# Ordering a router's experts on the chip and giving the 14 lightest a two-pass gate product

## The chip, the cores and the metric

The kernel runs on one core of one Trainium2 chip. The metric is the device time of one execution in microseconds, lower is better. Every time here comes from timed runs or from one execution that the hardware profiler recorded.

## What is computed

One decoder layer over 1024 tokens of width 1024: a mixer (gated linear attention beside differential attention), and then a mixture of experts. The change lies in the second part, which in the reference is this:

```python
def hier_moe(x, wg, bg, we, be, w1, w3, w2):
    ...
    g_w, g_idx = lax.top_k(g_prob, 1)                    # one of 4 groups
    e_w, e_idx = lax.top_k(jax.nn.softmax(e_sel, axis=-1), TOP_K)   # 2 of its 8 experts
    expert = g_idx * EXPERTS_PER_GROUP + e_idx
    ...
    def expert_block(args):
        xb, e = args
        hdn = jax.nn.silu(xb @ w1[e]) * (xb @ w3[e])     # 1024 -> 512, twice
        return hdn @ w2[e]                               # 512 -> 1024
    ...
    out = jnp.zeros((n_tok + 1, d), f32).at[row_tok].add(y.astype(f32) * row_w[:, None])[:n_tok]
```

Each token goes to 2 of 32 experts, so a list of tokens has 64 entries on average. With these inputs the reference's router gives lists of 34 to 88 tokens; experts 0 and 1 have 42 and 44, and the 14 lightest of the other 30 have 34 to 63.

## The kernel before

All is written with explicit semaphores; each engine has a program of its own. TensorE is PE, VectorE is DVE, ScalarE is ACT, GpSimd is POOL, and SP only issues transfers.

**The front.** The mixer, the router and the lists of tokens. `place[:, e, t]` says at which slot of expert e's list a token stands, `slot_rows` what is written there (token number and weight, in bf16 parts). It fills the first half of the span.

**The expert stage** (`stage_experts`, second half). `over_experts` runs the experts 0 to 31 in their own order: 4 written out, a loop over 24 in bodies of four, 4 written out, and a tail. Each engine's program of one expert is `pe_expert`, `act_expert`, `dve_expert`, `pool_expert`, `sp_expert`. Of one expert:

- Six chunks of weights of 1 MB (128 x 2048 fp32): 0, 1 of `w1`, 2, 3 of `w2` **of the expert before** and 4, 5 of `w3`. SP fetches a chunk of expert e once DVE has read the same chunk of expert e-2 (`load_chunk`, L1772).
- Products are made in fp32r with both operands split in two. ACT rounds a chunk to its high part (`high`, L1976, into `w_high`), DVE subtracts to get the low part (`low`, L1980, into `w_low`), PE multiplies. There are three slots of high and low parts, so ACT's rounding of a chunk waits until PE has used the chunk three before (`chunk_used`).
- A product (`product`) is three matmuls: x high by w high, x high by w low, x low by w high (L2003, L2004, L2005). The list of up to 96 slots is the stationary operand, 512 columns of weights are moving: 12 matmuls a chunk, 72 an expert.
- `silu` on ACT (L1931), `hidden` on DVE (L1935, `hd`), four transposes of `hd` on PE (`h_transposes`, L1907) between the gate products of chunks 0 and 1 of the next expert, split on ACT and DVE (L2167, L2236), the two `w2` chunks, `weighted` on ACT (`main_y`, L1938), and a scatter that adds 96 rows to `out` in memory (POOL, L1926).
- Ahead of that: for expert e+4 DVE makes the one-hot matrix of the list (`pick`, L1847), for e+3 PE turns it into token numbers (L1855), DVE adds them up (`main_token`, L1865) and POOL gathers the rows of x (L1892); for e+1 PE transposes them (L1900), and ACT and DVE split them (L2209, L2214).

DVE's order in expert e is what the prediction needs: `hd` of e-1, low 2, `hT_low`, low 3, low 4, weights and destinations of a list, two `xT_low`, token numbers, low 5, low 0 of e+1, `pick` of e+4, low 1 of e+1. It ends the stage's last expert in halves (`gate_by_half`, `h_half`, `down_by_half`). A list of over 96 would be done behind the tail; none is here.

Of the kernel before, what the change touches and what calls it, by code (L numbers as in the profile page):

```python
# [49 lines left out]
CAP = 96  # L50
MORE = -(-SEQ // CAP) - 1
# [27 lines left out]
EXPERTS = {"w_high1": 20, "w_high2": 28, "xT_high0": 36, "xT_high1": 39, "xT_low0": 42, "xT_low1": 45, "sl": 48,  # L79
# [31 lines left out]
def build(nc, a):  # L111
    with ExitStack() as top:
# [6 lines left out]
        def place(name, shape, dt=F32):  # L119
# [6 lines left out]
            "ident": keep("ident", [P, P]), "causal": keep("causal", [P, HG, 64]),  # L126
            "gain_q": keep("gain_q", [P, 1]), "gain_k": keep("gain_k", [P, 1]),
            "minus_half": keep("minus_half", [P, 8]),
            "logits": keep("logits", [P, T, NG + NE]),
            "dqT": place("dqT", [P, HD, SEQ]), "dkT": place("dkT", [P, HD, SEQ]),  # L130
# [88 lines left out]
def stage_front(nc, a, s, tools):  # L219
# [70 lines left out]
    e2, gexp = sb("e2", [P, 1], kib=19.1875), sb("gexp", [P, NG], kib=19.21875)  # L290
    w, wden = sb("w", [P, 2], kib=19.25), sb("wden", [P, 1], kib=19.28125)
# [55 lines left out]
    rel_out, filled, relf_mm, rel_step = sem("rel_out"), sem("filled"), sem("relf_mm"), sem("rel_step")  # L347
    lam_step, lam_exp, masked = sem("lam_step"), sem("lam_exp"), sem("masked")
    anti_ready, turned, prepared = sem("anti_ready"), sem("turned"), sem("prepared")
# [25 lines left out]
    placed, shared, weighed, flagged = sem("placed"), sem("shared"), sem("weighed"), sem("flagged")  # L375
    own = {"dve": 0, "pool": 0}
# [113 lines left out]
    def total_counts():  # L490

        nc.vector.tensor_copy(counts[:, 0:NE], pc[0:1, :])
        nc.vector.tensor_reduce(counts[:, NE:NE + 1], pc[0:1, :], AX.X, ALU.max)
# [10 lines left out]
    def sync(sp):  # L504
# [35 lines left out]
        sp.wait_ge(masked, 1)  # L540
# [51 lines left out]
        for n in range(1, T + 1):  # L592
# [3 lines left out]
            elif n == RING + 3:  # L596
                for c in range(2):
                    load_chunk(sp, a, s, 0, 0, c)
            elif n == T:
                sp.wait_ge(g_o_mm, T)  # L600
                for c in (0, 1):
                    load_chunk(sp, a, s, 1, 1, c)
                sp.wait_ge(added, 2 * T - 1)
                for c in (4, 5):
                    load_chunk(sp, a, s, 0, 0, c)
# [7 lines left out]
    def tensor(pe):  # L613
# [253 lines left out]
        nc.tensor.matmul(pf[:, 0:REL], relb[:], onehot[:], start=True, stop=True).then_inc(relf_mm, 1)  # L867
        for i in range(T, AHEAD):
# [6 lines left out]
            if 2 in behind.get(i, {}):  # L875
                if behind[i][2] == q_units[0]:
                    pe.wait_ge(rel_step, 1)
                q_transposes(behind[i][2])
            if i == INDEX["dv", 5]:
                pe.wait_ge(q_stored, T)  # L880
                pe.wait_ge(bias_in, 16 * HD)
                pe.wait_ge(anti_ready, 1)
# [60 lines left out]
    def scalar(act):  # L943
# [177 lines left out]
        for i in range(T, AHEAD):  # L1121
# [16 lines left out]
            if i == INDEX["z", 3]:  # L1138
                act.wait_ge(lam_step, 3)
                nc.scalar.activation(lexp[:], lsum[:], ACT.Exp).then_inc(lam_exp, 1)  # L1140
# [57 lines left out]
    def gpsimd(pool):  # L1198
# [33 lines left out]
        for half in range(2):  # L1232
# [3 lines left out]
                                    pattern=[[0, HG], [1, 64]],  # L1236
# [545 lines left out]
def stage_experts(nc, a, s, tools, front):  # L1782
# [209 lines left out]
    def sp_expert(sp, e, r, j, last, tail=False):  # L1992
        if not some(e, 2):
            return
# [553 lines left out]
```

## Time and profile before

| what | us |
|---|---|
| time, median of 3 runs | 1193.33 (1191.17 to 1193.42) |
| span of the profiled execution, first to last instruction | 1187.8 |
| PE busy in it | 1140.4 (96%) |
| DVE busy | 886.6 (75%) |
| ACT busy | 693.8 (58%) |
| POOL busy | 258.4 (22%) |

The span leaves out what lies around the program, 5.5 us against the median; a change of the span is taken as a change of the time. PE's busy time counts overlapping matmuls, so that a full PE says only that it is never empty. In the second half the DMA engines are busy without a pause as well. The rows of single instructions stand further below.

### The profile page before, as it was taken

The numbers are of one execution on the slowest core, as the hardware profiler recorded it, in microseconds if no ns is written. First come the engines' busy times: TensorE is split into PE (matmuls) and PEld (weight loads), VectorE is DVE, ScalarE is ACT, GpSimd is POOL, SyncE is SP. The second block draws the span as 40 slices with busy tenths as digits, with TensorE's granted clock in tenths as the row PEclk, the third lists the DMA queues.
The fourth block names the chain that finished last, engine by engine and source line by source line (L and its number), as shares of the span: only waits on it lengthen the run. The fifth ranks groups of instructions, "written<-read, shape, count | busy, mean of one in ns | idle before, by whom it ended". The sixth has DMA issues, their size and how long they took to land.

```text
span 1187.8 us, 17134 instructions
## 1 busy us (share of the span) xinstructions
PE 1140.4 (96%) x5899; PEld 866.7 (73%) x5900; DVE 886.6 (75%) x1304; ACT 693.8 (58%) x916; POOL 258.4 (22%) x327
## 2 busy tenths in 40 slices
PE   6999999999999889999699999999999999999997
PEld 5877887767777678888467777777777777777775
DVE  4424423666577788887699989999999999998885
ACT  5424203455455643434367777777777777777774
POOL 2211102411111222223441221212212122122111
PEclk9999999999999999999799999999999999999999
DMA  8130301200200444343599999999999999999982
GB/s 321 43 107 1 106 27 45 72 27 36 98 27 9 146 146 151 127 166 121 214 400 377 387 388 374 399 378 377 392 371 384 380 369 399 374 380 387 370 293 34
DMA packets 67794, 273.34 MB, mean 230 GB/s; under 512 B 13172, under 2 KB 19896, under 8 KB 43288
## 3 DMA queue, kind: packets, MB, share of 16 engines
q1 hardware_dynamic: 57000, 245.32, 53.4%
q0 software_dynamic: 7280, 20.98, 7.8%
q10 hardware_dynamic: 3456, 6.29, 1.4%
q8 instruction: 33, 0.54, 0.2%
q14 instruction: 25, 0.20, 0.1%
HBM read 248.44 MB, written 28.32 MB: 233 GB/s over the span
## 4 chain that ended last, share of the span: by engine, by line
PE 87%; DVE 6%; POOL 2%; ACT 2%; issue 2%; DMA 1%; POOLq 0%; ACTq 0%; DVEq 0%
PE main_pm L649 12%; PE main_score L649 6%; PE main_score L2003 5%; PE main_score L2005 5%; PE main_pt L2005 5%; PE main_score L2004 5%; PE main_pt L2003 5%; PE main_pt L2004 5%; PE main_po L2005 5%; PE main_po L2004 5%; PE main_po L2003 5%; PE main_score L710 3%; PE main_po L733 2%; PE main_score L821 2%; PE main_score L823 2%; PE main_score L822 2%
## 5 line engine op out<-in xcount | busy, mean ns | idle before, releaser
L1980 DVE TENSOR_TENSOR main_w_low<-w_raw,main_w_high 128x2048 fp32r<-128x2048 f32 x189 | 432.1, 2287 | 48.9 <-ACT main_w_high L1976 48.7
L1976 ACT CAST main_w_high<-w_raw 128x2048 fp32r<-128x2048 f32 x190 | 362.5, 1909 | 75.6 <-PE main_score L2005 52.6
L1892 POOL DMA_INDIRECT main_xg<-xn_dram,main_token x32 | 76.5, 2391 | 372.1 <-DVE main_token L1865 366.4
L2003 PE MATMUL main_score<-main_w_high,main_hT_high 128*96 128x512 f32 x256 | 102.4, 400 | 0.0
L2003 PE MATMUL main_pt<-main_w_high,main_xT_high 128*96 128x512 f32 x252 | 101.0, 401 | 0.0
L2005 PE MATMUL main_score<-main_w_high,main_hT_low 128*96 128x512 f32 x256 | 100.8, 394 | 0.0
L2004 PE MATMUL main_score<-main_w_low,main_hT_high 128*96 128x512 f32 x256 | 100.4, 392 | 0.0
L2005 PE MATMUL main_po<-main_w_high,main_xT_low 128*96 128x512 f32 (+1 forms) x256 | 100.3, 392 | 0.0
L2003 PE MATMUL main_po<-main_w_high,main_xT_high 128*96 128x512 f32 (+1 forms) x256 | 99.8, 390 | 0.2 <-DVE main_w_low L1980 0.2
L2005 PE MATMUL main_pt<-main_w_high,main_xT_low 128*96 128x512 f32 x252 | 99.8, 396 | 0.0
L2004 PE MATMUL main_po<-main_w_low,main_xT_high 128*96 128x512 f32 (+1 forms) x256 | 99.7, 389 | 0.0
L2004 PE MATMUL main_pt<-main_w_low,main_xT_high 128*96 128x512 f32 x252 | 98.9, 393 | 0.0
L649 PE MATMUL main_pm<-slot_high,xh 128*128 128x512 f32 x208 | 87.2, 419 | 2.5 <-DVE slot_low L1356 2.5
L649 PE MATMUL main_pm<-slot_low,xh 128*128 128x512 f32 x208 | 82.7, 398 | 0.0
L649 PE MATMUL main_pm<-slot_high,xl 128*128 128x512 f32 x208 | 82.4, 396 | 0.0
L1926 POOL DMA_INDIRECT out<-main_y,main_dest x31 | 50.4, 1627 | 90.0 <-ACT main_y L1938 52.4
L1011 ACT ACTIVATE main_prob<-main_score,main_nmax 128x128 f32<-128x128 f32 (+7 forms) x64 | 47.5, 743 | 32.8 <-DVE main_nmax L1415 32.0
L2004 PEld LDWEIGHTS main_po<-main_w_low,main_xT_high 128*96 128x96 f32 x256 | 41.4, 162 | 17.7
L2005 PEld LDWEIGHTS main_score<-main_w_high,main_hT_low 128*96 128x96 f32 x256 | 41.2, 161 | 17.9
L2003 PEld LDWEIGHTS main_po<-main_w_high,main_xT_high 128*96 128x96 f32 x256 | 41.3, 161 | 17.5 <-DVE main_w_low L1980 0.4
L2005 PEld LDWEIGHTS main_po<-main_w_high,main_xT_low 128*96 128x96 f32 x256 | 41.3, 161 | 17.3
L2005 PEld LDWEIGHTS main_pt<-main_w_high,main_xT_low 128*96 128x96 f32 x252 | 40.6, 161 | 17.7
(329 smaller groups left out, 2333.7 us busy)
## 6 DMA issues: line engine op xcount, KB each, us to landing
w_raw<-in_moe_w SPq DMA_DIRECT2D x192, 1024.0 KB, 18.0
slot_raw<-in_w_in SPq DMA_DIRECT2D x12, 1024.0 KB, 7.4
main_x<-in_x SPq DMA_DIRECT2D x8, 512.0 KB, 11.0
slot_raw<-in_w_out SPq DMA_DIRECT2D x4, 1024.0 KB, 6.8
main_hx<-in_x SPq DMA_DIRECT2D x8, 512.0 KB, 3.8
out<-main_hx SPq DMA_DIRECT2D x8, 512.0 KB, 2.9
xn_dram<-main_xn SPq DMA_DIRECT2D x8, 512.0 KB, 2.8
gr_dram<-main_stage ACTq DMA_DIRECT2D x8, 256.0 KB, 2.0
```

Of the source, the lines that this page charges most:

```text
L649: last = nc.tensor.matmul(bank(i), stationary, moving, start=(k == 0 and n == 0), stop=(k == KD - 1 and n == 2))
L710: last[comp] = nc.tensor.matmul(score[comp][:, k0:k1], dqT[r:r + 64, h, t * P:(t + 1) * P], dkT[r:r + 64, h, k0:k1], start=True, stop=True)
L733: last = nc.tensor.matmul(po[:, 0:DDV], wT[:, j, :], dv[:, j, h * DDV:(h + 1) * DDV], start=(j == 0), stop=(j == t))
L821: nc.tensor.matmul(acc[half], hi, w_hi, start=(k == 4), stop=False)
L1011: nc.scalar.activation(out, score[comp][:, 0:nk], ACT.Exp, bias=nmax[:, n % 2, comp:comp + 1], accum_out=sums[:, n % 3, comp:comp + 1]).th ...
L1892: nc.gpsimd.indirect_dma_start(xg[u][:], None, s["xn2_dram"], bass.IndirectOffsetOnAxis(token[u][:, 0:1], 0), bounds_check=bound["x"], oob ...
L1926: nc.gpsimd.indirect_dma_start(a["out"].rearrange("b n d -> (b n) d"), bass.IndirectOffsetOnAxis(dest[v][:, 0:1], 0), y[u][:], None, bound ...
L1976: nc.scalar.copy(wh[slot(c, e)][:], raw[u][c // 2][:, c % 2, :]).then_inc(w_high, 1)
L1980: nc.vector.tensor_tensor(wl[slot(c, e)][:], raw[u][c // 2][:, c % 2, :], wh[slot(c, e)][:].bitcast(F32), ALU.subtract).then_inc(w_low, 1)
L2003: nc.tensor.matmul(out, x_hi, w_hi, start=start, stop=False)
L2004: nc.tensor.matmul(out, x_hi, w_lo, start=False, stop=False)
L2005: return nc.tensor.matmul(out, x_lo, w_hi, start=False, stop=stop)
```

## The change

After the router the 32 experts are ordered by their number of tokens: experts 0 and 1 stay first, the others follow, the heaviest first. DVE multiplies the counts by 32 and takes off the expert's number to get different keys, compares each with each, PE counts by products with ones who stands above whom, and DVE turns this into `order`. SP and POOL read `order` into a register for each expert (`ranked`, `value_load`) and take weights and lists by it. POOL copies the expert's `place` and `slot_rows` to `place_of` and `rows_of`, from which DVE's `pick` and PE's product then read (`list_rows`).

The first 18 of the order are done as before ("heavy"). The last 14 ("light") take lists of 64. Their x stands in one tile `xT_both` of 128 columns, 64 high parts beside 64 low parts, so that a gate chunk takes 8 matmuls, by `w_high` and by `w_low`, and not 12. The result has 128 rows; ACT copies both gate results to `both`, and PE multiplies them by `fold`, a matrix of zeros and ones that adds row n+64 to row n and transposes at once. ACT then takes the silu of the first, DVE multiplies, and both split the hidden values. Products with `w2` are as before; the scatter writes 64 rows.

```diff
+    def compare(dve):
+        ...
+        dve_then(dve, V.scalar_tensor_tensor(out=key[:], in0=pc[0:NE, :], scalar=float(NE), in1=s["key_bias"][0:NE, :],
+                                             op0=ALU.mult, op1=ALU.add))
+        ...
+        V.tensor_scalar(above[:], key[:], key_at[:, 0:1], None, ALU.is_lt).then_inc(order_step, 1)
...
+    xTb = [sb(f"xT_both{u}", [P, KD, 2 * LIGHT_CAP], F32R, kib=EXPERTS[f"xT_high{u}"]) for u in range(2)]
+    both = [sb(f"both{m}", [P, DE], kib=EXPERTS[n]) for m, n in enumerate(("sl", "hd"))]
...
+    def fold_mm(pe, m, by_block=False):
+        for j in range(KE):
+            h = both[m][:, j * P:(j + 1) * P] if by_block else both[m].rearrange("p (c k) -> p k c", k=KE)[:, j, :]
+            last = nc.tensor.matmul(folded[m][:, j, :], h, fold[:], start=True, stop=True)
+        return last
...
+        if isinstance(e, int) and e == 2:
+            sp.wait_ge(after["order_step"], after["ORDERED"])
+        which = None if tail else ranked(sp, e)
...
+    def ranked(eng, e):
+        return eng.value_load(s["order"][0:1, bass.ds(e, 1)], min_val=0, max_val=NE - 1)
...
+            if light:
+                nc.tensor.matmul(ph_both[c // 4], xTb[u][:, kx, :], w_hi[:, w], start=(kx == 0), stop=False)
+                last = nc.tensor.matmul(ph_both[c // 4], xTb[u][:, kx, :], w_lo[:, w], start=False,
+                                        stop=(kx == KD - 1))
...
+            act.wait_ge(chunk_used, number(e - 1, 5) + 1)
+            nc.scalar.copy(both[1][:], ph_both[1]).then_inc(q.hd, 1)
...
+    def turned_hidden(dve, e):
+        dve.wait_ge(slT_ready, folds(e))
+        nc.vector.tensor_tensor(hT[:], folded[1], slT[:], ALU.mult).then_inc(hT_ready, 1)
+        dve.wait_ge(hT_high, e)
+        nc.vector.tensor_tensor(hTl[:, :, 0:LIGHT_CAP], hT[:], hTh[:, :, 0:LIGHT_CAP].bitcast(F32),
+                                ALU.subtract).then_inc(hT_low, 1)
...
         if not last:
-            pick(q, e + 4, e + 4, u)
+            dve.wait_ge(listed_rows, e + 3)
+            pick(q, e + 4, e + 4, u, place_of[u][:])
...
+    def list_rows(pool, e, u):
+
+        which = ranked(pool, e)
+        if some(e, 4):
+            pool.wait_ge(q.ids_mm, e - 1)
+        nc.gpsimd.tensor_copy(place_of[u][:], place[:, bass.ds(which, 1), :].rearrange("p a t -> p (a t)"))
+        nc.gpsimd.tensor_copy(rows_of[u][:], rows[:, :, bass.ds(which, 1), :].rearrange(
+            "p t a r -> p t (a r)")).then_inc(listed_rows, 1)
...
         if not (tail or (last and j >= 1)):
             pool_gather(pool, e + 3, 1 - u)
+        if not last:
+            list_rows(pool, e + 4, u)
...
+        four_of(0, 0, False)
+        with eng.Fori(1, 4) as i:
+            four_of(4 * i, 2 * i, False, light=False)
+        four_of(16, 8, False)
+        with eng.Fori(5, NE // 4 - 1) as i:
+            four_of(4 * i, 2 * i, False, light=True)
+        four_of(NE - 4, NE // 2 - 2, True)
+        expert(eng, NE, NE // 2, 0, True, [True, False, False], tail=True)
```

The last expert's gate and hidden product are no longer done in halves.

**POOL, one expert in the loop.** Of before, the gather of a list and the scatter of the one that is done:

```order
L2293 REGISTER_ALU
L1890 REGISTER_ALU
L1892 DMA main_xg_167<-xn_dram,main_token_187 96x1024
L2302 ISA
L1923 ISA
L1926 DMA out<-main_y_209,main_dest_189 1024x1024
```

Of the changed kernel, where between the two a register is loaded and two copies read what the front left in SBUF:

```order
L1949 DMA main_xg_172<-xn_dram,main_token_192 96x1024
L2073 ISA
L2073 TENSOR_LOAD order
L2073 ISA x2
L2381 ISA
L2381 COPY main_place_of_219<-place 128x8
L2382 ISA
L2382 COPY main_rows_of_217<-slot_rows 128x48
L1987 REGISTER_ALU
L1990 DMA out<-main_y_225,main_dest_196 1024x1024
```

The copies stand behind the gather and ahead of the scatter; nothing of this was on POOL in the loop before.

**DVE, from low 5 of an expert to `hT_low` in the next.** Of before:

```order
L1980 TENSOR_TENSOR main_w_low_176<-w_raw_66,main_w_high_172 128x2048
L1980 TENSOR_TENSOR main_w_low_170<-w_raw_67,main_w_high_168 128x2048
L1847 TENSOR_TENSOR main_onehot_180<-iota_slot,place 128x768
L1980 TENSOR_TENSOR main_w_low_171<-w_raw_67,main_w_high_169 128x2048
L1935 TENSOR_TENSOR main_hd<-main_po,main_sl 96x512
L1980 TENSOR_TENSOR main_w_low_176<-w_raw_68,main_w_high_172 128x2048
L2236 TENSOR_TENSOR main_hT_low<-main_score,main_hT_high 128x384
```

Of the changed kernel, in the loop over light experts:

```order
L2046 TENSOR_TENSOR main_w_low_182<-w_raw_69,main_w_high_178 128x2048
L2045 ISA
L2046 TENSOR_TENSOR main_w_low_176<-w_raw_64,main_w_high_174 128x2048
L1903 TENSOR_TENSOR main_onehot_187<-iota_slot,main_place_of_219 128x768
L2046 TENSOR_TENSOR main_w_low_177<-w_raw_64,main_w_high_175 128x2048
L2045 REGISTER_ALU
L2046 TENSOR_TENSOR main_w_low_182<-w_raw_65,main_w_high_178 128x2048
L2293 REGISTER_ALU
L2294 TENSOR_TENSOR main_hT<-main_score,main_slT 128x256
L2296 TENSOR_TENSOR main_hT_low<-main_hT,main_hT_high 128x4x64
```

The one-hot matrix is now made from POOL's copy; in a light expert `hd` is gone and a product of 128x256 stands behind low 2. In a heavy expert `hd` stays where it was.

## Rows read from the trace of the kernel before

**Rows 1.** The page: busy time of each engine.

```profile
PE 1140.4 (96%) x5899; PEld 866.7 (73%) x5900; DVE 886.6 (75%) x1304; ACT 693.8 (58%) x916; POOL 258.4 (22%) x327
```

**Rows 2.** Stretches: length, busy us (instructions) of the five, PE's clock, DMA share, GB/s.

```profile
711.00:715.00 4.00, 4.00 (x19) 2.81 (x18) 3.62 (x4) 3.57 (x4) 2.51 (x2) 1.00 1.01 426
700.00:1100.00 400.00, 400.00 (x2004) 291.29 (x2004) 365.69 (x327) 307.93 (x263) 83.98 (x44) 1.00 1.02 382
```

**Rows 3.** Groups, 700 to 900 us, shapes apart: busy, mean ns, idle before and releasers.

```profile
L1980 DVE TENSOR_TENSOR main_w_low<-w_raw,main_w_high 128x2048 fp32r<-128x2048 f32 x66 | 150.9, 2287 | 16.8 <-ACT main_w_high L1976 16.8
L1976 ACT CAST main_w_high<-w_raw 128x2048 fp32r<-128x2048 f32 x66 | 126.0, 1909 | 27.0 <-PE main_score L2005 19.3 <-PE main_po L2005 7.7
...
L1847 DVE TENSOR_TENSOR main_onehot<-iota_slot,place 128x768 bf16<-128x768 f32 x11 | 10.5, 951 | 0.0
...
L2214 DVE TENSOR_TENSOR main_xT_low<-main_pm,main_xT_high 128x384 fp32r<-128x384 f32 x11 | 6.0, 547 | 0.0
```

**Rows 4.** Timeline of one expert: start, duration, instruction, idle before and releaser.

```profile
850.04 0.59 ACT L1931 ACTIVATE main_sl<-main_pt 96x512 f32<-96x512 f32 x1 [0.50 <-PE main_pt L2005]
...
858.80 2.29 DVE L1980 TENSOR_TENSOR main_w_low<-w_raw,main_w_high 128x2048 fp32r<-128x2048 f32 x1 [0.39 <-ACT main_w_high L1976]
...
861.01 0.95 DVE L1847 TENSOR_TENSOR main_onehot<-iota_slot,place 128x768 bf16<-128x768 f32 x1
861.88 2.28 DVE L1980 TENSOR_TENSOR main_w_low<-w_raw,main_w_high 128x2048 fp32r<-128x2048 f32 x1
...
862.22 0.39 PE L2003 MATMUL main_pt<-main_w_high,main_xT_high 128*96 128x512 f32 x1
862.45 0.39 PE L2004 MATMUL main_pt<-main_w_low,main_xT_high 128*96 128x512 f32 x1
...
864.08 0.68 DVE L1935 TENSOR_TENSOR main_hd<-main_po,main_sl 96x512 f32<-96x512 f32 x1
...
864.81 0.20 PEld L1907 LDWEIGHTS main_score<-ident,main_hd 96*128 96x128 f32 x1
...
868.43 0.59 ACT L1931 ACTIVATE main_sl<-main_pt 96x512 f32<-96x512 f32 x1 [0.49 <-PE main_pt L2005]
```

**Rows 5.** Timeline of POOL's gather in that expert.

```profile
857.01 2.26 POOL L1892 DMA_INDIRECT main_xg<-xn_dram,main_token  x1 [13.00 <-DVE main_token L1865]
```

**Rows 6.** Timeline at the start of the stage, POOL beside DVE.

```profile
588.70 2.47 POOL L498 CAST slot_rows<-main_weight 128x32 bf16<-128x32 f32 x1 [3.30 <-DVE main_weight L487]
...
591.59 0.29 POOL L500 CAST slot_rows<-main_weight 128x32 bf16<-128x32 f32 x1
...
588.75 2.27 DVE L1980 TENSOR_TENSOR main_w_low<-w_raw,main_w_high 128x2048 fp32r<-128x2048 f32 x1
```

**Rows 7.** By line: a register load on POOL; columns: duration ns min/median/max, start.

```profile
L2396 POOLq TENSOR_LOAD <-counts x1: 510/510/510, 1181.0 to 1181.0; - x1
```

**Rows 8.** Timeline rows of like shapes: 128-row stationary, fp32 products, 256 columns on DVE.

```profile
547.68 0.39 PE L821 MATMUL main_score<-slot_high,main_o_high 128*128 128x512 f32 x1
547.91 0.39 PE L822 MATMUL main_score<-slot_low,main_o_high 128*128 128x512 f32 x1
...
561.87 1.87 PE L839 MATMUL main_score<-main_w_router,main_hxT 128*128 128x36 f32 x16
...
1171.02 0.41 DVE L2225 TENSOR_TENSOR main_hd<-main_po,main_sl 96x256 f32<-96x256 f32 x1
```

**Rows 9.** DMA, 700 to 1100 us: queue's packets, MB, share; issues with us to landing.

```profile
q0 software_dynamic: 4829, 14.45, 15.3%
...
w_raw<-in_moe_w SPq DMA_DIRECT2D x130, 1024.0 KB, 18.2
```

**Rows 10.** DMA, 1133.9 to 1134.9 us: the last `w3` chunk's issue.

```profile
w_raw<-in_moe_w SPq DMA_DIRECT2D x1, 1024.0 KB, 15.2
```

**Rows 11.** Timeline of the end: that chunk's rounding on ACT, POOL's last scatter.

```profile
1164.66 3.72 ACT L1976 CAST main_w_high<-w_raw 128x2048 fp32r<-128x2048 f32 x2 [0.43 <-PE main_score L2005]
...
1181.68 1.41 POOL L1916 DMA_INDIRECT out<-main_y,main_dest_odd  x1 [0.30 <-issue]
```

More of the change, by code:

```diff
@@ L2118, in pe_x, with pe_expert @@
         x_transposes(pe, q, e, u, 16 * (r + 1))
-    def pe_expert(pe, e, r, j, last, tail=False):
+    def pe_expert(pe, e, r, j, last, light, tail=False):
         u = j % 2
@@ L2136, in pe_expert @@
             pe.wait_ge(q.silu, e)
-            gate(pe, e, 0, u)
-            h_transposes(pe, q, e - 1)
-            gate(pe, e, 1, u)
+            gate(pe, e, 0, u, light[1])
+            if light[0]:
+                if isinstance(e, int) and e == HEAVY + 1:
+                    pe.wait_ge(after["filled"], 13)
+                pe.wait_ge(q.hd, e)
+                fold_mm(pe, 0)
+                fold_mm(pe, 1).then_inc(q.h_mm, 1)
+            else:
+                h_transposes(pe, q, e - 1)
+            gate(pe, e, 1, u, light[1])
             if not (last and j == 3):
@@ L2143, in pe_expert @@
                 pe_ids(pe, e + 3, 1 - u)
-        if not tail:
             pe.wait_ge(hT_low, e)
-        if some(e, 2):
+            if isinstance(e, int) and e == 1:
+                pe.wait_ge(after["order_step"], after["ORDERED"])
+            if some(e, 2):
+                pe.wait_ge(q.y_ready, 2 * e - 2)
+            down(pe, e, 2)
+            down(pe, e, 3)
+            pe.wait_ge(q.hd, e)
+            gate(pe, e, 4, u, light[1])
+            gate(pe, e, 5, u, light[1])
+        else:
+            pe.wait_ge(q.hd, e)
+            fold_mm(pe, 0, by_block=True)
+            fold_mm(pe, 1, by_block=True).then_inc(q.h_mm, 1)
+            pe.wait_ge(hT_low, e)
@@ L2177, in act_expert @@
                 act.wait_ge(q.hd, e)
-            silu(act, q)
+            if light[1]:
+                nc.scalar.copy(both[0][:], ph_both[0]).then_inc(q.silu, 1)
+            else:
+                silu(act, q)
             if some(e, 1):
@@ L2219, in dve_expert @@
+    def turned_hidden(dve, e):
[4 more added lines that the diff above has]
+                                ALU.subtract).then_inc(hT_low, 1)
+    def dve_expert(dve, e, r, j, last, light, tail=False):
         u = j % 2
         if tail:
-            dve.wait_ge(q.silu, NE)
@@ L2230, in dve_expert @@
-            return
-        if some(e, 1):
+            turned_hidden(dve, e)
+            low(dve, e, u, 3)
+            return
+        if light[0]:
+            low(dve, e, u, 2)
+            turned_hidden(dve, e)
+            low(dve, e, u, 3)
+        elif some(e, 1):
             dve.wait_ge(chunk_used, number(e - 1, 5) + 1)
@@ L2335, in tensor @@
             list_tokens(pe, e)
+        pe.wait_ge(after["added"], 2 * T)
+        front["rank"][1](pe)
+        front["rank"][3](pe)
         pe_x(pe, 0, 0, 0)
@@ L2353, in gpsimd @@
             front["own"]["pool"] += 1
+        pool.wait_ge(after["logits_mm"], T)
+        nc.gpsimd.memset(fold[:], 0.0).then_inc(after["filled"], 1)
+        for n in range(2):
+            pool.wait_ge(after["filled"], n + 11)
+            nc.gpsimd.affine_select(out=fold[:], in_=fold[:], compare_op=ALU.not_equal, fill=1.0, base=-LIGHT_CAP * n,
+                                    pattern=[[-1, LIGHT_CAP]], channel_multiplier=1).then_inc(after["filled"], 1)
         front["weights"](pool, T - 1)
+        pool.wait_ge(after["weighed"], T)
+        pool.wait_ge(after["order_step"], after["ORDERED"])
+        for e in (2, 3):
+            list_rows(pool, e, e % 2)
         pool_gather(pool, 2, 0)
```

274 lines of the change are left out of this document (143 added, 131 removed).

## The prediction

> **What bounds the kernel now.** I read the busy times first [rows 1]: PE is busy 96% of the span, but its matmuls overlap, so this only says that it is never empty. The stretches come next [rows 2]. From 700 to 1100 us PE's clock is 1.00, its full 2.4 GHz, and the DMA share is 1.02 at 382 GB/s. Two resources look full, and the timeline tells which one is waited for. ACT's silu stands at 850.04 and again at 868.43 [rows 4]: an expert takes 18.39 us. PE issues a matmul of 512 columns every 0.23 us there [rows 4], 72 of them are 16.6 us, and transposes and list products fill the rest. In the groups ACT's idle time is ended by PE [rows 3], never by a transfer. A chunk of weights lands 18.2 us after its issue [rows 9]; the last `w3` chunk was issued near 1134.2 and landed 15.2 later [rows 10], at 1149.4, and ACT began on it behind 1164.66, in the second of two roundings joined in one row [rows 11], so near 1166. So data lie ready some 15 us: PE is the bound, with a DMA system that has nothing to spare behind it. DVE is busy 365.69 of 400 us [rows 2], 16.8 of 18.39 an expert. It also holds the one hand-over without slack: `hd` runs from 864.08 to 864.76, and PE loads its transposes at 864.81 [rows 4], right behind the last matmul of chunk 0.
>
> **What a light expert saves.** Its four gate chunks drop 16 of 72 matmuls, 16 x 0.231 = 3.7 us. That 128 stationary rows and not 96 slow nothing is seen where they follow each other by 0.23 us, 547.68 and 547.91 [rows 8]. Eight fold products replace four transposes; the nearest row has 16 fp32 products of 36 columns in 1.87 us [rows 8], 0.12 each, so the fold is about 1.0 against 0.4. PE would need 18.39 - 3.7 + 0.55 = 15.25 us.
>
> PE does not get to set that pace, DVE does. DVE keeps six subtractions of 2.29 [rows 3]. It loses `hd` (0.68 [rows 4]), and three of 128x384 at 0.55 [rows 3], 2.3 together, and gains a product, a hidden subtraction and two `xT` of 256 columns at some 0.4 each (0.41 for 96x256 [rows 8]), 1.6. That is 16.8 - 0.7 = 16.1. The new chain makes DVE wait once: between its product and its subtraction ACT must round, and ACT has a rounding of 1.91 us [rows 3] in its order ahead of that. DVE is then a subtraction behind ACT, so I take 0.6 of it, with 0 and 1.9 as bounds. Light: 16.7 us, 1.7 less than now. ACT swaps silu and three casts for two copies and smaller ones, from 307.93/400 x 18.39 = 14.2 [rows 2] to about 14.7, under DVE.
>
> **What every expert pays.** `pick` now waits for POOL's two copies. POOL gathers from 857.01 to 859.27 [rows 5], then loads a register (0.51 [rows 7]) and comes to its first copy near 860.0. At that time DVE subtracts low 0, from 858.80 to 861.09 [rows 4]. The start of the stage shows what this does: a POOL cast that takes 0.29 us elsewhere took 2.47, from 588.70 to 591.17, while DVE's subtraction ran from 588.75 to 591.02 [rows 6]. It was held until DVE was done, and ended 0.15 later. The Trainium skill, page "SBUF — State Buffer", section "Who interferes with whom", has this as a rule: a VectorE instruction with two inputs in SBUF and a GpSimd instruction that reads SBUF exclude each other, and the later one waits for all of the earlier. By that rule, and it speaks against this change, the copies cannot be hidden beside low 0; the trace's 2.47 beside 2.27 agrees.
>
> So the first copy ends at 861.09 + 0.15 = 861.24 and the second, at 0.29 [rows 6] plus a small gap, near 861.57, and `pick` starts at 861.62 in place of 861.01: w = 0.6. The bounds are 0 (a small copy finished before 861.01) and 1.4 (the register load is held as well: 861.09 + 0.51 + 0.2 + 0.6 = 862.4). Behind `pick` in DVE's order stand low 1 and `hd` of the expert before, and for `hd` PE waits at once. With 0.1 slack each heavy expert from 1 to 17 loses 0.5: 17 x 0.5 = 8.5. Of the light ones 18 to 27 still make a `pick`, so their 16.7 becomes 17.3 and they save 1.1: 10 x 1.1 = 11. The last four make none: 4 x 1.7 = 6.8.
>
> **Front and end.** The ordering is a dozen DVE and PE operations of 0.15 to 0.3 each in a stretch where both wait for gathers; the loads of expert 2 need it at 588, when it is over. What counts is that POOL makes the copies for lists 2 and 3 where DVE wants to `pick` (593.99), behind weights that are late by the held cast: +1.5, bounds 0 and 3. At the end the halves are gone, and copy, fold, silu, product, two roundings and 24 matmuls stand in a row where the halves overlapped: about +1.0, bounds 0 and 3.
>
> **Transfers.** They set a floor. Weights alone go at 426 GB/s [rows 2], 6.29 MB in 14.8 us; the rest of 18.39, 3.6, is for 160 gathered and scattered rows. 32 fewer save 0.72 (by q0's share of 15.3% [rows 9] it is 2.8 x 32/160 = 0.56). Eleven light scatters lie ahead of the last `w3` chunk, 7.9, and one more comes to lie ahead of it, 1.4. It would land 6.5 earlier, at 1142.9. Rounding and subtraction (4.5) and the chain from gate product to end (about 19.5) make 1167: 21 us under today's span. Nothing can be faster than that unless transfers are. The Trainium skill, page "DMA: Bandwidth & Descriptors", section "Bandwidth", gives a core some 358 GB/s from memory; by it a light expert's 6.8 MB would take 19 us and the change gain nothing. The trace shows 382 over 400 us, so I follow the trace and keep it as part of a rival.
>
> **The sum.** -11 - 6.8 + 8.5 + 1.5 + 1.0 = -6.8. Against the span of 1187.8 this is 1181.0; against the median, which lies 5.5 higher, 1186.5. In terms of w it is 27 w - 23: each tenth of a microsecond that `pick` waits costs 2.7.
>
> **The rivals.**
> - *The wait is small and transfers bind.* If POOL gets its copies through before low 0 or between instructions, w is 0 and the sum -17 - 6.8 + 2.5 = -21, just what the transfers allow: 1172 to 1174. For it speaks that 13 of POOL's 18 us are idle [rows 5]; against it that the copies stand in order behind a gather which waits for its tokens.
> - *Slower: the copies cost more.* The place is `pick` in experts 1 to 27. It decides from w = 0.85 on, where 27 w eats the 23. If the register load is held too, w = 1.4 and the sum is +14.8: 1208. For it: POOL then has load and two copies all behind 861.09. Against it: a load is the sequencer's and need not use the port.
> - *No gain from light lists, no loss in heavy ones.* If DVE's wait for ACT is 1.9 and not 0.6, light experts take 18.6 with `pick` and 18.0 without; with w = 0.6 the heavy ones' 8.5 stay, and the sum is near +11. With half of that wait it is about zero: 1193. The page's 358 GB/s comes to about this as well.
> - *PE sets the pace.* 14 x 3.1 = 43 less, 1152. DVE's 16.1 of work and the transfers stand against it.
>
> **Chances and range.** 1187 with its own range 1180 to 1194: 0.45. Small wait, 1173: 0.22. Slower by dear copies, 1208: 0.20. No effect, 1193: 0.10. PE's pace: 0.03. Within 0.2% (2.4 us, about what this kernel's measurement can tell from no change, 1190.9 to 1195.7) lie 0.07 of the first case and most of the fourth: 0.13. Faster: 0.36 of the first, the second and the last, 0.62. Slower: 0.25. For 8 in 10 the range takes the small wait and half of the dear copies: 1171 to 1204.
>
> **What would show it.** In heavy experts a period of 18.9 between silus, DVE idle by 0.6 ahead of the one-hot matrix, released by POOL, and POOL's first copy ending 0.15 behind low 0. Light experts at 17.3 with DVE over 90% busy and PE under it. Landings rising above 18.2 us, and ACT waiting for DMA, would mean that transfers bind. I am wrong if copies are hidden (faster), if DVE waits for ACT in the fold chain by more than 0.6 (slower), or if the light pace is that of the transfers.

## The result and the profile after

The changed kernel takes 1220.26 us (median of 4 runs, 1218.89 to 1221.63) against 1193.3 for the kernel before: ratio 1.0238, 95% interval 1.0223 to 1.0253. It is slower by 2.4%, outside the stated range of 1171 to 1204. Its profiled execution has a span of 1219.8 us, 32.0 longer than that of before.

The page gives the engines' busy times, answering to [rows 1]:

```profile
PE 1157.8 (95%) x5822; PEld 893.0 (73%) x5823; DVE 882.8 (72%) x1309; ACT 697.8 (57%) x943; POOL 329.5 (27%) x394
```

PE has 77 matmuls fewer than before and is busy 17 us longer. Where, the stretches say (columns as in [rows 2]); the first two hold heavy experts, the last one light ones, and the third passes from one kind to the other:

```profile
700.00:800.00 100.00, 99.91 (x491) 71.13 (x490) 91.10 (x80) 75.20 (x64) 36.78 (x24) 1.00 1.02 384
800.00:900.00 100.00, 99.91 (x502) 71.75 (x501) 90.26 (x79) 76.01 (x66) 32.30 (x20) 1.00 1.02 377
900.00:1000.00 100.00, 96.98 (x454) 74.99 (x453) 85.58 (x83) 73.03 (x67) 33.19 (x20) 0.95 1.01 375
1000.00:1100.00 100.00, 96.81 (x448) 77.67 (x447) 83.29 (x76) 72.97 (x71) 33.93 (x21) 0.95 0.97 343
```

In the light stretch DVE falls to 83% and the transfers to 343 GB/s. Their share is still 0.97, but a chunk of weights now lands 7.2 us after its issue, and not 18.2 as before [rows 9], and from 600 us on ACT waits for no transfer. So neither binds. The issues of 950 to 1110 us, with KB and median us to landing:

```profile
w_raw<-in_moe_w SPq DMA_DIRECT2D x49, 1024.0 KB, 7.2
```

PE is busy for 97%, at a mean clock of 0.95, and its weight loads (PEld) are busier than in heavy experts although there are fewer. The timeline of PE in one light expert shows both. Rows are start, duration, instruction; chunk 0's last products, the fold, chunk 1's first:

```profile
1004.82 0.50 PE L2088 MATMUL main_pt<-main_w_high,main_xT_both 128*128 128x512 f32 x1 [0.70 <-DVE main_w_low L2046]
...
1006.56 0.40 PE L2089 MATMUL main_pt<-main_w_low,main_xT_both 128*128 128x512 f32 x1
1006.57 3.81 PEld L1972 LDWEIGHTS main_score<-main_fold,main_both 128*128 128x128 f32 x16
1006.80 3.72 PE L1972 MATMUL main_score<-main_fold,main_both 128*128 128x64 f32 x16
...
1010.33 0.53 PE L2088 MATMUL main_pt<-main_w_high,main_xT_both 128*128 128x512 f32 x1
...
1012.79 0.63 PE L2088 MATMUL main_pt<-main_w_high,main_xT_both 128*128 128x512 f32 x1
1012.79 0.33 PEld L2089 LDWEIGHTS main_pt<-main_w_low,main_xT_both 128*128 128x128 f32 x1
1013.21 0.63 PE L2089 MATMUL main_pt<-main_w_low,main_xT_both 128*128 128x512 f32 x1
```

The fold is 8 products in the code and 16 in the record: each is done in two passes. They take from 1006.80 to 1010.33, where chunk 1 starts: 3.53 us, 0.22 a pass. The prediction had 1.0. (A row's own duration runs to the end of its last pass, which overlaps what follows.) Behind it a product of 512 columns follows the last by 0.43 us (1012.79, 1013.21) and not by 0.23. The stretches of the fold and of chunk 1 say why:

```profile
1006.80:1010.30 3.50, 3.50 (x17) 3.50 (x17) 3.50 (x2) 0.86 (x1) 0.49 (x1) 1.00 1.03 331
1010.30:1013.60 3.30, 3.30 (x9) 2.50 (x10) 1.04 (x4) 2.47 (x3) 0.00 (x0) 0.55 1.04 365
```

The granted clock is 1.00 through the fold and 0.55 behind it, near the 1.2 GHz level. So it went behind 8 of the first 12 folds: chunk 1 takes 3.0 to 3.5 us there and 1.92 behind the other four. (Behind the fold in the last expert's program it takes 3.2 to 3.5 in all kernels that have one there, at a clock of 1.00 too; it is left out of these counts.)

The fourteenth fold stands in the tail, where the code takes the stationary operand in blocks of neighbours (`by_block=True`) even in the changed kernel:

```profile
1200.23 2.00 PE L1972 MATMUL main_score<-main_fold,main_both 128*128 128x64 f32 x16 [0.68 <-ACT main_both L2224]
```

Its 16 passes follow each other by 0.11 us, half of what the strided ones take. So one trace holds both ways of reading side by side.

ACT, which makes the silu of the folded values, waits 2.9 us an expert for the fold. A weight load of the fold takes 327 ns on the mean; the groups of 950 to 1120 us (columns as in [rows 3]):

```profile
L1972 PEld LDWEIGHTS main_score<-main_fold,main_both 128*128 128x128 f32 x128 | 30.5, 327 | 0.3
...
L2229 ACT ACTIVATE main_slT<-main_score 128x256 f32<-128x256 f32 x9 | 3.5, 383 | 26.1 <-PE main_score L1972 26.1
```

In a heavy expert, POOL and DVE where `pick` stands:

```profile
849.22 2.33 DVE L2046 TENSOR_TENSOR main_w_low<-w_raw,main_w_high 128x2048 fp32r<-128x2048 f32 x1 [0.38 <-ACT main_w_high L2042]
849.69 1.90 POOL L2381 COPY main_place_of<-place 128x8 f32 x1
851.55 0.21 POOL L2382 COPY main_rows_of<-slot_rows 128x48 bf16 x1
851.79 0.96 DVE L1903 TENSOR_TENSOR main_onehot<-iota_slot,main_place_of 128x768 bf16<-128x768 f32 x1 [0.25 <-POOL main_rows_of L2382]
```

The first copy, 0.19 us where DVE is still, takes 1.90 and ends with DVE's subtraction, at 851.59 beside 851.55. DVE then idles 0.25 us, released by POOL. And the start of the stage: ACT's silu, which marks an expert as in [rows 4], the copy for the fourth list, and DVE's one-hot matrix of the fifth, which waits for copies that stand behind two gathers:

```profile
594.93 0.59 ACT L1995 ACTIVATE main_sl<-main_pt 96x512 f32<-96x512 f32 x1 [5.42 <-PE main_pt L2078]
595.26 3.27 POOL L2381 COPY main_place_of<-place 128x8 f32 x1 [0.43 <-issue]
...
608.89 0.96 DVE L1903 TENSOR_TENSOR main_onehot<-iota_slot,main_place_of 128x768 bf16<-128x768 f32 x1 [1.23 <-POOL main_rows_of L2382]
...
616.26 0.59 ACT L1995 ACTIVATE main_sl<-main_pt 96x512 f32<-96x512 f32 x1 [0.51 <-PE main_pt L2078]
```

The 32.0 us by stretches. The marks are the second expert's silu, the eighteenth's, the first light fold and the thirteenth, and the end of the span; before, the first two stand at 611.0 and 905.2, and the 12 periods are taken at 18.39:

| stretch | before | after | more |
|---|---|---|---|
| to the second expert's silu | 611.0 | 616.3 | 5.3 |
| 16 heavy periods | 294.2 (18.39 each) | 298.9 (18.69 each) | 4.7 |
| 12 periods between light folds | 220.7 | 237.1 (19.76 each) | 16.4 |
| the rest: passage to light experts, and end | 61.9 | 67.5 | 5.6 |

### The profile page after: what moved, and what is told of

Read it like the earlier page. It is cut to its first block, busy times and chain, and to the rows that moved or that the text cites. A ratio compares the mean times of both kernels' runs of the same rounds, so it can differ in the third digit from the quotient of the medians.

```text
span 1219.8 us, 17253 instructions
## 1 busy us (share of the span) xinstructions
PE 1157.8 (95%) x5822; PEld 893.0 (73%) x5823; DVE 882.8 (72%) x1309; ACT 697.8 (57%) x943; POOL 329.5 (27%) x394
## 4 chain that ended last, share of the span: by engine, by line
PE 80%; DVE 9%; ACT 4%; issue 3%; POOL 2%; DMA 1%; POOLq 0%; ACTq 0%; DVEq 0%
PE main_pm L693 12%; PE main_score L693 6%; PE main_score L2076 5%; PE main_score L2078 5%; PE main_score L2077 5%; PE main_score L1972 4%; DVE main_w_low L2046 3%; PE main_pt L2088 3%; PE main_score L754 3%; PE main_pt L2078 3%; PE main_pt L2076 3%; PE main_pt L2077 3%; PE main_po L2076 3%; PE main_po L2078 3%; PE main_po L2077 3%
## 5 line engine op out<-in xcount | busy, mean ns | idle before, releaser
L2088 PE MATMUL main_pt<-main_w_high,main_xT_both 128*128 128x512 f32 x112 | 52.6, 470 | 7.9 <-DVE main_w_low L2046 7.9
L2078 PE MATMUL main_po<-main_w_high,main_xT_low 128*96 128x512 f32 x144 | 57.9, 402 | 0.0
L2076 PE MATMUL main_po<-main_w_high,main_xT_high 128*96 128x512 f32 x144 | 57.7, 401 | 0.0
L2077 PE MATMUL main_po<-main_w_low,main_xT_high 128*96 128x512 f32 x144 | 57.6, 400 | 0.0
L2076 PEld LDWEIGHTS main_score<-main_w_high,main_hT_high 128*96 128x96 f32 x256 | 41.8, 163 | 21.2 <-DVE main_hT_low L2296 5.2
L2076 PE MATMUL main_pt<-main_w_high,main_xT_high 128*96 128x512 f32 x140 | 56.3, 402 | 0.0
L2078 PE MATMUL main_pt<-main_w_high,main_xT_low 128*96 128x512 f32 x140 | 55.4, 396 | 0.0
L2381 POOL COPY main_place_of<-place 128x8 f32 x30 | 55.0, 1834 | 1.5 <-POOL slot_rows L546 1.0
L2077 PE MATMUL main_pt<-main_w_low,main_xT_high 128*96 128x512 f32 x140 | 55.0, 393 | 0.0
L2077 PEld LDWEIGHTS main_score<-main_w_low,main_hT_high 128*96 128x96 f32 x256 | 41.8, 163 | 15.8 <-issue 0.2
```

The source lines that it names most:

```text
L2076: nc.tensor.matmul(out, x_hi, w_hi, start=start, stop=False)
L2077: nc.tensor.matmul(out, x_hi, w_lo, start=False, stop=False)
L2078: return nc.tensor.matmul(out, x_lo, w_hi, start=False, stop=stop)
L2088: nc.tensor.matmul(ph_both[c // 4], xTb[u][:, kx, :], w_hi[:, w], start=(kx == 0), stop=False)
L2381: nc.gpsimd.tensor_copy(place_of[u][:], place[:, bass.ds(which, 1), :].rearrange("p a t -> p (a t)"))
```

## The experiments

All compare against the kernel before, timed on the same chip (its medians there: 1191.2, 1190.3 and 1192.9 us).

**The fold reads neighbours.** The strided operand of the fold is written apart by ACT, in the copy that is made anyway:

```diff
-                fold_mm(pe, 0)
-                fold_mm(pe, 1).then_inc(q.h_mm, 1)
+                fold_mm(pe, 0, by_block=True)
+                fold_mm(pe, 1, by_block=True).then_inc(q.h_mm, 1)
...
-            nc.scalar.copy(both[1][:], ph_both[1]).then_inc(q.hd, 1)
+            if tail:
+                nc.scalar.copy(both[1][:], ph_both[1]).then_inc(q.hd, 1)
+            else:
+                nc.scalar.copy(both[1].rearrange("p (k c) -> p k c", k=KE),
+                               ph_both[1].rearrange("p (c k) -> p k c", k=KE)).then_inc(q.hd, 1)
```

The copy to `both[0]` is changed in the same way. The last expert keeps its plain copies; its fold read neighbours already.

> Same results. ACT's two copies of the gate results write each block of 128 hidden columns side by side, so that the fold's stationary operand is read as 128 neighbours and not as every fourth element. Theory (the light period is PE's, and the strided weight load is what makes the fold 3.5 us): the 16 fold passes go from 0.22 to 0.11 us each, 1.7 less per light expert, 12 of them: -21, 1199; if the fall of the granted clock behind the fold goes too, about 1.3 more in 9 of them: -12 more, 1187. Rival A (transfers set the light pace of 19.8): 1220, the fold shorter and an idle PE in its place. Rival B (two passes of fp32 cost 0.22 whatever the stride): fold stays at 3.5, 1220.

1188.45 us, ratio 0.9976 (0.9963 to 0.9989), 32 less than the changed kernel. One light expert in its timeline:

```profile
1031.28 1.99 PEld L1972 LDWEIGHTS main_score<-main_fold,main_both 128*128 128x128 f32 x16
1031.51 1.90 PE L1972 MATMUL main_score<-main_fold,main_both 128*128 128x64 f32 x16
1033.21 0.48 PE L2088 MATMUL main_pt<-main_w_high,main_xT_both 128*128 128x512 f32 x1
```

The same 16 passes take from 1031.51 to 1033.21, 1.70 us. Chunk 1 behind takes 1.94 in all 12 experts, so the clock no longer falls. The light period is 17.2. ACT's rearranged copy costs what the plain one did (0.58 to 0.59). Both rivals of the expectation fall: transfers do not hold the light pace, and two passes of fp32 do not cost 0.22 of themselves.

**POOL copies ahead of the gather.** `list_rows(pool, e + 4, u)` stands before `pool_gather(pool, e + 3, 1 - u)` in POOL's program of an expert:

```diff
-        if not (tail or (last and j >= 1)):
-            pool_gather(pool, e + 3, 1 - u)
         if not last:
             list_rows(pool, e + 4, u)
+        if not (tail or (last and j >= 1)):
+            pool_gather(pool, e + 3, 1 - u)
```

> Same results. POOL's two copies stand ahead of the gather in its order. Theory (in heavy experts `pick` waits for copies that are held by DVE's subtraction): the heavy period goes from 18.69 back to 18.39, 16 x 0.3 = -4.8; the light ones, bound by PE, keep 19.8; the start gains up to 2: 1213 to 1216. Rival (the copies disturb DVE wherever they stand, or the 0.3 comes from the register loads): 1220.

1210.74 us, ratio 1.0158 (1.0137 to 1.0179), somewhat better than expected. POOL and DVE at `pick`, in a heavy expert:

```profile
846.07 0.95 DVE L1903 TENSOR_TENSOR main_onehot<-iota_slot,main_place_of 128x768 bf16<-128x768 f32 x1
847.01 2.26 POOL L2381 COPY main_place_of<-place 128x8 f32 x1
849.22 0.21 POOL L2382 COPY main_rows_of<-slot_rows 128x48 bf16 x1
```

The copy is held for 2.26 us, longer than the 1.90 above, but nobody waits for it, and DVE has no idle time ahead of the one-hot matrix. The heavy period is 18.39 again. The rest of the gain over my 1213 to 1216 is the clock: it fell in 5 of 12 light experts here. Without its fall the light period is 19.01, with it 20.15.

**Both edits.**

> Same results. Both edits together. Theory: they lie on different experts, so the gains add, -26 to -38: 1182 to 1194. If with the short fold DVE's order binds the light experts, the copies' place is worth something there too, up to 0.4 x 10 more. Rival A (transfers): 1215.

1180.28 us, ratio 0.9907 (0.9889 to 0.9925): a version faster than the kernel before. Light periods are 17.15, heavy ones 18.39, and the second silu stands at 610.9. Its light stretch, 950 to 1120 us:

```profile
950.00:1120.00 170.00, 164.66 (x868) 127.25 (x867) 158.64 (x149) 142.31 (x139) 69.02 (x35) 1.00 1.02 392
```

DVE is busy 93%, the clock 1.00, and the transfers run at 392 GB/s, more than before. In 950 to 1110 us a chunk lands 23.3 us after its issue, later than the 18.2 of before, and still ACT waits for no transfer.

**The ordering and the copies without light lists.** All but the last expert are heavy:

```diff
-HEAVY = 18
+HEAVY = 31
...
-            four_of(4 * i, 2 * i, False, light=True)
+            four_of(4 * i, 2 * i, False, light=False)
```

> Same results. 31 experts are done as heavy, only the last as light: the ordering and POOL's copies without light lists. Theory: start +5, 28 periods at 18.69 in place of 18.39 +8.4, end about +1: 1193 + 14.5 = 1208. Rival (the loss of the changed kernel lies in the ordering, its register loads and the order of transfers, and grows with the expert's number): 1215 or more.

1205.71 us, ratio 1.0121 (1.0102 to 1.014). The period is 18.69 from the second expert's silu to the last `pick`, as expected, and does not grow with the expert's number. By its trace the ordering costs 2.9 us up to the second silu, 8.0 in these periods, by the copies' place, and 4.2 behind them, where the halves are gone.

**The last chain in another order.** x3_both, with ACT rounding the last chunk before it copies the gate result, and DVE subtracting it before the hidden product:

```diff
+        if tail:
+            high(act, e, r, u, 3)
         if light[0]:
             act.wait_ge(chunk_used, number(e - 1, 5) + 1)
...
-            turned_hidden(dve, e)
             low(dve, e, u, 3)
+            turned_hidden(dve, e)
             return
```

> Same results. x3_both, and behind the last expert ACT rounds its last chunk ahead of copying the gate result, in 1.6 us in which it is idle, and DVE subtracts it ahead of the hidden product. Theory: the last chain (fold, silu, product, rounding, subtraction) no longer waits for ACT's rounding of 1.9, PE's idle 3.0 shrinks by 1.1, the rest of the chain is unchanged: 1179. Rival (the copy of the gate result comes later by what the rounding overlaps, 0.2 to 0.6): no change, 1180.

1177.79 us, ratio 0.9907 (0.9892 to 0.9922), the same ratio as x3_both's. In the traces the stretch from the last silu to the end is 16.4 in place of 17.9 us. A gain of that size is a tenth of a per cent and the ratios do not tell it.

**A fold in one pass.** x3_both with both operands rounded to fp32r (the gate results lose their low bits):

```diff
-    both = [sb(f"both{m}", [P, DE], kib=EXPERTS[n]) for m, n in enumerate(("sl", "hd"))]
+    both = [sb(f"both{m}", [P, DE], F32R, kib=EXPERTS[n]) for m, n in enumerate(("sl", "hd"))]
...
+        nc.gpsimd.tensor_copy(fold_r[:], fold[:]).then_inc(after["filled"], 1)
...
-            last = nc.tensor.matmul(folded[m][:, j, :], h, fold[:], start=True, stop=True)
+            last = nc.tensor.matmul(folded[m][:, j, :], h, fold_r[:], start=True, stop=True)
```

> x3_both with the fold's two operands rounded to fp32r, so that 8 products take 8 passes and not 16 (the gate results lose their low bits there). Theory P (the light period of 17.15 is a ring: last w2 chunk used, ACT rounds chunk 0, DVE subtracts, PE does chunk 0, fold, chunk 1, lists, w2 chunks; 4.45 + 12.7): the fold's 0.85 less comes off in full or until another limit is met, 16.3 to 16.9, 1169 to 1177. Theory D, as the prediction had it (DVE's work and its waits set 17.2): less than 0.1 each, 1179 to 1180. Floor by transfers: about 1170.

1173.9 us, ratio 0.9871 (0.9855 to 0.9887), the lowest ratio here, though its interval overlaps with those of two kernels below. The light period is 16.81 in most experts. Who is waited for there:

```profile
1017.68 0.50 PE L2089 MATMUL main_pt<-main_w_high,main_xT_both 128*128 128x512 f32 x1 [0.35 <-DVE main_w_low L2047]
1018.41 4.49 DVE L2047 TENSOR_TENSOR main_w_low<-w_raw,main_w_high 128x2048 fp32r<-128x2048 f32 x2
1019.61 0.97 PE L1973 MATMUL main_score<-main_fold_rounded,main_both 128*128 128x64 f32 x8
1020.75 0.51 PE L2089 MATMUL main_pt<-main_w_high,main_xT_both 128*128 128x512 f32 x1 [0.17 <-DVE main_w_low L2047]
...
1024.35 0.47 PE L2077 MATMUL main_score<-main_w_high,main_hT_high 128*96 128x512 f32 x1 [0.29 <-DVE main_hT_low L2304]
```

The fold ends 0.8 earlier than in two passes, and PE now waits for DVE in three places: low 0 as before, low 1 (which stands behind `pick`), and the low hidden parts. Of 0.8 less on PE 0.35 come off the period. Neither theory of the expectation holds alone: at 17.15 the light expert is set by PE and by the hand-over to DVE in turn, with a third of a microsecond to the next limit. Weights are near as well: ACT waits for a transfer once, 0.7 us.

**One pass, read by fours.** x2_copies_first with the same rounding, so that 8 passes read every fourth element.

> x2_copies_first with the fold's operands rounded to fp32r, read as every fourth element as in the changed kernel: 8 passes with slow weight loads (the gate results lose their low bits there). If the stride makes each load slow, the fold takes 8 x 0.22 = 1.8 us, as in x3_both, 1180. If the granted clock falls because of strided loads as such, chunk 1 behind it still takes 3.2 us in most light experts, and the time is 1190 or more; if it falls because the thin work lasts 3.5 us, it does not fall, and 1180 holds. If the stride costs nothing with one pass, the fold takes 0.9 and the time is that of x6_fold_one_pass.

1177.69 us, ratio 0.9897 (0.9881 to 0.9913). One fold:

```profile
1039.92 1.83 PE L1973 MATMUL main_score<-main_fold_rounded,main_both 128*128 128x64 f32 x8
```

Chunk 1 starts at 1041.58. The fold takes 1.66 us, 0.21 a pass, so the step is what slows a pass. The clock does not fall in any expert.

**Copies twice.** The changed kernel; POOL makes both copies first into tiles that nobody reads:

```diff
+        nc.gpsimd.tensor_copy(spare_place[u][:], place[:, bass.ds(which, 1), :].rearrange("p a t -> p (a t)"))
+        nc.gpsimd.tensor_copy(spare_rows[u][:], rows[:, :, bass.ds(which, 1), :].rearrange("p t a r -> p t (a r)"))
         nc.gpsimd.tensor_copy(place_of[u][:], place[:, bass.ds(which, 1), :].rearrange("p a t -> p (a t)"))
```

> Same results. The changed kernel, POOL makes both copies twice (the first time into tiles that nobody reads). Theory (`pick` waits for the copies, each 0.2 us once DVE's subtraction is done): w grows by 0.4 to 0.5 in each heavy expert, 17 x 0.45 = +7.7, in light ones (PE's pace) 0 to 0.4: 1228, up to 1232. Rival (the first copy is held, all later ones slip in free while DVE is at other work): 1220 to 1222.

1227.22 us, ratio 1.031 (1.0278 to 1.0341).

```profile
850.93 1.90 POOL L2383 COPY main_spare_place<-place 128x8 f32 x1
852.78 0.21 POOL L2384 COPY main_spare_rows<-slot_rows 128x48 bf16 x1
852.95 0.18 POOL L2385 COPY main_place_of<-place 128x8 f32 x1
853.08 0.21 POOL L2386 COPY main_rows_of<-slot_rows 128x48 bf16 x1
853.32 0.96 DVE L1905 TENSOR_TENSOR main_onehot<-iota_slot,main_place_of 128x768 bf16<-128x768 f32 x1 [0.54 <-POOL main_rows_of L2386]
```

DVE's wait grows from 0.25 to 0.54 and the heavy period from 18.69 to 18.98: every tenth that `pick` waits is a tenth of the period. Of the 7 us between the medians, 17 x 0.29 = 4.9 are this. The rest is not placed: the two profiled spans differ by 4.1, and the kernel's runs lie between 1222 and 1230.

**The fold done twice.** x3_both, with the 16 passes over neighbours repeated:

```diff
-                fold_mm(pe, 0, by_block=True)
-                fold_mm(pe, 1, by_block=True).then_inc(q.h_mm, 1)
+                for again in range(2):
+                    fold_mm(pe, 0, by_block=True)
+                    done = fold_mm(pe, 1, by_block=True)
+                done.then_inc(q.h_mm, 1)
```

> Same results. x3_both with the fold's 16 passes done twice over, all with neighbouring columns: 3.4 us of thin products, as long as the strided fold of the changed kernel. If the clock falls because thin work lasts that long, chunk 1 behind it takes 3.0 to 3.5 us in most light experts, the light period is 19 to 20, and the time 1180 + 13 x 1.7 + 9 x 1.2 = 1213. If slow strided loads are what it takes, the clock stays at full speed, chunk 1 takes 1.94, the period is 18.85 and the time 1202. If the ring of PE and the hand-over did not set the light period, 1180 to 1185.

1203.67 us, ratio 1.0092 (1.0071 to 1.0113). The stretches of fold and chunk 1:

```profile
1014.80:1018.30 3.50, 3.50 (x34) 3.50 (x32) 3.29 (x2) 0.91 (x1) 3.37 (x2) 1.00 1.04 311
1018.30:1020.24 1.94, 1.94 (x11) 1.59 (x11) 0.42 (x1) 1.73 (x2) 0.00 (x0) 1.00 1.02 304
```

It is as long as the strided fold, 3.49 us, and the clock stays at 1.00 in all 12 experts. The period is 18.93: 1.79 us more on PE put 1.78 on the period.

**Seventeen heavy experts.** x5_tail_order with `HEAVY = 17`.

> Same results. x5_tail_order with 17 heavy and 15 light experts (the one that moves has 63 tokens). Theory: one period of 18.39 becomes one of 17.15: 1.2 less than x5_tail_order, ratio to before 0.9897. Rival (the order's change of one list costs as much): 0.9907.

1177.75 us, ratio 0.9873 (0.9853 to 0.9892). The ratio is below x5_tail_order's by more than was expected, the time itself is the same; the intervals meet at 0.9892. In the traces the stretch from the second silu to the end is 563.2 us in place of 564.3. So the gain is there, and by the traces it is about the 1.2 expected.

**Which products the step slows.** The transposes of the kernel before read `hd` with the same step, at 0.12 us or less. Two kernels, each x2_copies_first with another fold (the first leaves out the low parts of 32 tokens, the second folds nothing):

```diff
+            rows_in = P if by_block else CAP
+            last = nc.tensor.matmul(folded[m][:, j, :], h[0:rows_in], fold[0:rows_in, :], start=True, stop=True)
```

> x2_copies_first with the fold taken over 96 of the 128 rows, every fourth element as before (the low parts of 32 tokens are left out). The transposes of the kernel before read `hd` with the same step of four on 96 rows, at 0.11 us each. If the full 128 rows are what makes a strided load slow, the passes take 0.11 here too, the fold 1.7 to 1.8, the time about 1180; if the step of four slows any load outside transposes, they stay at 0.22, the fold at 3.5, the time 1210.

```diff
+                last = nc.tensor.transpose(banks["pt"][:, j * P:(j + 1) * P], h, ident[:])
```

> x2_copies_first with eight plain transposes of 128 rows, every fourth element, in place of the eight fold products (nothing is folded, and the second four overwrite the first: the hidden values are not those of the reference). If the mode decides, a transpose takes 0.11 us, the eight 0.9; if 128 strided rows do, 0.22, the eight 1.8. Time 1172 to 1180.

1214.04 and 1173.86 us, one run each. The first's fold, then the second's:

```profile
1016.02 3.81 PEld L1973 LDWEIGHTS main_score<-main_fold,main_both 96*128 96x128 f32 x16
1016.25 3.72 PE L1973 MATMUL main_score<-main_fold,main_both 96*128 96x64 f32 x16
```

```profile
1019.26 1.16 PEld L1975 LDWEIGHTS main_score<-ident,main_both 128*128 128x128 f32 x8
1019.49 1.12 PE L1975 MATMUL main_score<-ident,main_both 128*128 128x128 f32 x8
```

With 96 rows a pass still takes 0.22 us, and the clock fell in 10 of 12 experts. The eight transposes of 128 rows by fours start 0.12 us apart. So the number of rows is not what slows a pass, and in a transpose the step does not. The two kinds also differ in the moving operand, 64 columns against 128; why a transpose is spared is open.

## Why the prediction was wrong

**The step that failed** is the fold's size: "the nearest row has 16 fp32 products of 36 columns in 1.87 us [rows 8], 0.12 each, so the fold is about 1.0". The fold took 3.53 us, and what followed it was slower too. The step was wrong three times, always low.

1. *Products and passes.* The row counts passes. The router's line stands in a loop of 8 products, and the record has 16. Eight fold products are 16 passes, 1.70 us at 0.11 (x1_block_fold). The row named the price of a pass; I took it for that of a product.
2. *The step of four.* The router's operands are neighbours, the fold's stationary operand is every fourth fp32. That makes a pass 0.22 and the fold 3.53: 1.83 more, and the period went from 19.01 (x2_copies_first, no clock fall) to 17.15 (x3_both) when it was taken away. The changed kernel's own tail agrees, 0.11 a pass over neighbours. x9_fold_twice, x11_fold_96 and x12_fold_transposed bound it: the length of PE's work counts in full, 96 rows are no faster, a transpose takes 0.12. The four transposes that the fold replaced had the same step at 0.12 or less, and so made the step look free. The Trainium skill, page "SBUF — State Buffer", section "Door 1: The DMA port swizzle", has that SBUF is read in lines of 16 bytes, that each access which crosses to a new line pays, and that fp32 can be strided up to 4 for free. The runs agree that a step of 16 bytes pays in a product, 0.22 against 0.11 us, and disagree that 4 is free; in a transpose it was.
3. *The clock.* It fell behind the strided fold in 8 of 12 experts, to 0.51 to 0.61 over chunk 1, and about 1.15 us came on top (20.15 against 19.01). It fell with 16 strided passes (in 8, 5, 8 and 10 of 12 experts in the four kernels that have them) and in those 12 experts never with 16 or 32 passes over neighbours, 8 strided ones or 8 transposes. What in the strided passes brings the fall, and why it comes behind some folds and not behind others, is open. I had kept PE's clock at 1.00 throughout.

Term by term, against the sum in the prediction:

- *Light experts, -17.8.* Measured 12 periods of 19.76 in place of 18.39, and not 17.3. With the fold read by neighbours they are 17.15. So all else of this term (16 matmuls fewer, DVE's order, the wait on ACT) came out nearly right as a sum. Not so as a mechanism: I had PE at 15.25 and DVE setting 17.3. In x3_both PE is taken up for 16.6 us and idles 0.55 ahead of chunk 0. With the fold at 1.7 my sum for PE would have been 15.95. The rest is not in it: the list products take 0.58 with the wait behind them, and not 0.34, chunk 5 loses 0.28 at its start, and chunk 0 another 0.11 behind the idle time. The idle time comes from a ring. The rounding of chunk 0 waits for the slot that the last `w2` chunk leaves, and rounding and subtraction (1.9 + 2.3) are longer than chunks 4 and 5 of a light expert (3.7) that cover them; x3_both:

```profile
1032.34 1.91 ACT L2042 CAST main_w_high<-w_raw 128x2048 fp32r<-128x2048 f32 x1 [0.86 <-PE main_score L2078]
1034.29 2.29 DVE L2046 TENSOR_TENSOR main_w_low<-w_raw,main_w_high 128x2048 fp32r<-128x2048 f32 x1 [0.21 <-ACT main_w_high L2042]
1036.63 0.50 PE L2088 MATMUL main_pt<-main_w_high,main_xT_both 128*128 128x512 f32 x1 [0.40 <-DVE main_w_low L2046]
```

x9_fold_twice and x6_fold_one_pass show the two sides: longer PE work counts in full, shorter by less than half. The agreement of 17.3 with 17.15 was luck: experts that make no `pick` were to take 16.7, and the last periods of x3_both are 17.1 as well.
- *The copies, +8.5.* The mechanism is as forecast, DVE's and POOL's exclusion included, and the size was about half: `pick` waited 0.25 and not 0.6, and a heavy expert lost 0.30 and not 0.5, 4.7 in all. The first copy ends with the subtraction and not 0.15 behind it, and the second takes 0.21. The register load, my rival's ground, was long done: it stands at 847.30, ahead of the gather's end, and takes 0.29. Moving the copies takes 18.69 to 18.39, doubling them makes it 18.98.
- *The front, +1.5.* Measured 5.3. POOL's copy for the fourth list took 3.27 us, beside a one-hot matrix and a subtraction of DVE. The copies for the fifth list then kept DVE waiting 1.23. From the first silu to the second it is 17.4 us before, 21.3 after, 21.4 to 21.9 in the three other kernels with the copies behind the gather, and 17.7 to 20.3 with them ahead; what makes it vary there is open.
- *The end, +1.0.* Too small. In the table above passage and end are 5.6 us longer. In x3_both the stretch from the last heavy silu to the end saves 11.2 us where 14 experts at 1.24 would give 17.4, so passage and end cost 6.2. In the tail PE idles 3.0 us while the hidden values are made, and then runs near half clock; the stretch of x3_both:

```profile
1162.00:1166.00 4.00, 4.00 (x11) 2.62 (x10) 1.70 (x1) 0.00 (x0) 0.00 (x0) 0.54 0.00 0
```

- *Transfers.* No run met the floor, a span of 1167: the light stretch ran at 392 GB/s in x3_both, and x6_fold_one_pass came to a span of 1170.9 with one wait for weights, 0.7 us. The Trainium skill's 358 GB/s (page "DMA: Bandwidth & Descriptors", section "Bandwidth") was passed here as well. That section gives it as a core's share when both cores of a memory domain stream; here one core ran.

**The rivals.** The time is slower, but not by the mechanism that I gave for slower: dear copies would have made heavy experts 19.7. A dearer fold was no rival at all. I had one for PE setting the pace, on the fast side only, and never asked what a slower PE would give, though the one operation that no row of before showed in its shape was PE's.

## What to carry to other kernels

Count a record's instructions against the loop in the code before dividing by them; an fp32 product is two here. A DMA share near 1 does not say that transfers bind: at 0.97 the weights landed 7.2 us after their issue, and nobody waited for them. Give the operand that no row shows in its shape and step a bound from both sides, above all on the engine that is never empty: in x9_fold_twice each microsecond added to PE was a microsecond of the period. And where work has to be copied anyway, let the copy lay it out for its reader; it cost ACT nothing and took 32 us off.

## What the runs showed of the hardware

- An ordinary product whose stationary operand is every fourth fp32 takes 0.22 us a pass and not 0.11, with two passes or one, with 96 rows or 128. Its weight load takes 0.33 and not 0.19. A transpose with the same step takes 0.12.
- PE's clock was granted at 1.00 through 3.49 us of 64-column passes over neighbours and behind it, and fell to 0.51 to 0.66, the mean over chunk 1, behind 3.53 us of strided ones in 31 of 48 cases (four kernels). Why behind some and not behind others of one execution is open.
- A POOL copy of 128x8 takes 0.19 us alone and 1.4 to 3.3 beside DVE's subtractions, and ends within 0.05 us of them.
